# State-space heads: the skip term as a matrix product, the gate in one step, scores in their own bank

## What is computed

```python
cb = jnp.einsum('bclgn,bcsgn->bcgls', cm, bm)                       # scores of a group
y_diag = jnp.einsum('bcgrls,bcsgrp->bclgrp', cb[:, :, :, None] * jnp.exp(seg), xd)
y_off = jnp.einsum('bcqgn,bcgrpn->bcqgrp', cm, h_in) * jnp.exp(a_cs)[..., None]
y = y_f + flip(y_b) + d_skip[:, None] * xs                          # skip term
y = y.reshape(b, l, D_SSD) * jax.nn.silu(z)                         # gate
return rmsnorm(y, norm_w), h_f, h_b
```

## Time and profile before

| | us |
|---|---|
| median of 3 runs | 1427.8 (1423.75 to 1427.95) |
| profiled execution | 1429.21 |
| its span in the trace | 1427.4 |
| busy in the span: TensorE, VectorE, ScalarE, GpSimd | 1308.0, 794.8, 610.0, 88.7 |
| mean granted TensorE clock | 0.972 |

### The profile page before, as it was taken

The page is one execution under the profiler, slowest core; times in us unless marked ns, Lnnn a source line. Parts: engine busy times, 40 slices in busy tenths (PEclk is TensorE's granted clock), DMA queues, the critical chain, the costliest instruction groups (busy, mean ns, idle before and its releaser), DMA issues.

```text
span 1427.4 us, 26314 instructions
## 1 busy us (share of the span) xinstructions
PE 1308.0 (92%) x11170; PEld 1108.6 (78%) x11170; DVE 794.8 (56%) x1220; ACT 610.0 (43%) x947; POOL 88.7 (6%) x69
## 2 busy tenths in 40 slices
PE   7999999999999999999999999899978777877777
PEld 7989698999989988999989999588544334444535
DVE  5558857877467587777458796874222111222214
ACT  6553346444456686454446654763211111121112
POOL 2000000300003100020000000410000000000000
PEclk9999999999999999999999999899998989899999
DMA  9655357554574567445562050468999999999996
GB/s 371 246 206 200 139 216 284 206 190 177 183 312 167 210 251 294 179 177 185 199 240 96 34 236 1 163 266 342 427 428 428 427 429 429 427 429 425 427 428 267
DMA packets 30359, 383.32 MB, mean 269 GB/s; under 512 B 3552, under 2 KB 3728, under 8 KB 7216
## 3 DMA queue, kind: packets, MB, share of 16 engines
q1 hardware_dynamic: 29504, 377.72, 65.2%
q0 software_dynamic: 752, 4.11, 0.7%
HBM read 380.77 MB, written 1.05 MB: 267 GB/s over the span
## 4 chain that ended last, share of the span: by engine, by line
PE 64%; DMA 24%; DVE 6%; ACT 4%; issue 1%; POOL 0%; SPq 0%; DVEq 0%; ACTq 0%; POOLq 0%
PE ps L699 63%; DMA ring<-in_experts 24%; DVE work L2023 2%; DVE w_lo L2011 2%; ACT w_hi L1463 1%; ACT work L1463 1%; ACT HM L1463 1%; DVE work L2011 1%; DVE HM L2011 0%; PE ps L858 0%; DVE SQ L2017 0%; DVE sg_lo L2011 0%; DVE small L2187 0%; DMA ring<-in_dense 0%; ACT L1463 0%
## 5 line engine op out<-in xcount | busy, mean ns | idle before, releaser
L2011 DVE TENSOR_TENSOR w_lo<-ring,w_hi 128x1024 fp32r<-128x1024 f32 (+1 forms) x273 | 338.2, 1245 | 202.9 <-ACT w_hi L1463 202.7
L1463 ACT ACTIVATE w_hi<-ring 128x1024 fp32r<-128x1024 f32 (+1 forms) x273 | 287.0, 1055 | 262.8 <-PE ps L699 258.9
L699 PE MATMUL ps<-in_hi,w_hi 128*128 128x256 f32 x1376 | 388.2, 282 | 11.2 <-DVE w_lo L2011 10.2
L699 PE MATMUL ps<-in_hi,w_lo 128*128 128x256 f32 x1376 | 385.1, 280 | 0.0
L699 PE MATMUL ps<-in_lo,w_hi 128*128 128x256 f32 x1376 | 385.1, 280 | 0.0
L699 PE MATMUL ps<-ring,work 128*32 128x256 f32 (+3 forms) x2520 | 206.0, 460 | 80.9 <-DMA ring<-in_experts 72.6
L699 PEld LDWEIGHTS ps<-in_hi,w_hi 128*128 128x128 f32 x1376 | 261.1, 190 | 15.6 <-issue 13.6
L699 PEld LDWEIGHTS ps<-in_lo,w_hi 128*128 128x128 f32 x1376 | 261.0, 190 | 0.2
L699 PEld LDWEIGHTS ps<-in_hi,w_lo 128*128 128x128 f32 x1376 | 261.1, 190 | 0.0
L699 PEld LDWEIGHTS ps<-ring,work 128*32 128x32 f32 (+1 forms) x2520 | 84.3, 118 | 185.4 <-issue 109.2
L2023 DVE SCALAR_TENSOR_TENSOR X<-ps,mod,X 128x256 f32<-128x256 f32 x136 | 59.0, 479 | 249.7 <-PE ps L699 249.6
(11 more groups left out here) (291 smaller groups left out, 1890.8 us busy)
## 6 DMA issues: line engine op xcount, KB each, us to landing
ring<-in_experts SPq DMA_DIRECT2D x89, 2048.0 KB, 23.1
ring<-in_dense SPq DMA_DIRECT2D x82, 2048.0 KB, 7.5
ring<-in_experts SPq DMA_DIRECT2D x5, 512.0 KB, 20.9
work<-in_experts SPq DMA_DIRECT2D x1, 2048.0 KB, 13.4
ring<-in_dense SPq DMA_DIRECT2D x3, 512.0 KB, 7.2
spare<-in_experts SPq DMA_DIRECT2D x1, 1536.0 KB, 10.6
cst<-in_ret_cst POOLq DMA_DIRECT2D x1, 1280.0 KB, 13.3
cst<-in_experts SPq DMA_DIRECT2D x1, 1280.0 KB, 5.6
```

The costliest lines, as they stand in the source:

```text
L699: i = pe.matmul(o, l, r, start=start, stop=stop)
L1463: x = act.activation(o, i, f, **kw)
L2011: i = dve.tensor_tensor(out=o, in0=x, in1=y, op=op)
```

## The change

- `y`: TensorE first adds the identity times `xs_lat` to the pair's bank, the 12 products accumulate on it. `xs_lat` has been multiplied by `d_skip` in place on ScalarE, eight copies between gating tile 3 and the last two Fourier outputs (`skip_ready`).
- `y_out`: one VectorE step, PSUM times gate into `xs_lat`. Its readers wait for the bank's read count in place of `y_ready`, SP among them.
- Scores: `cb` goes to bank `MODB` with semaphores `cb_full` and `cb_read`; these tiles leave the rotating sequence, so later tiles have lower numbers.
- Squares: `y_square(0)` and `(1)` come after the clamps of heads 8 and 12, `(2)` after head 15; `y_sums(0)` and `(1)` after pairs 4 and 6, `(2)` with `(3)` after the first blocks of the projection.
- States: ScalarE splits the weights first and reads states 0 and 1; VectorE copies states 2 and 3 after its remainders. Pair 0 waits for all four.
- Start-up semaphores `ones_set`, `csil_zero` and `pads_zero` become counts 1, 2 and 3 of `fills`. Their list and three waits are left out of the diff.

```diff
--- before.py
+++ after.py
@@ -216,7 +216,7 @@
         _tiles("state", SG_)
     elif _kind == "mix":
         _seq.append(("mix_out", _i))
-    else:
+    elif _kind != "cb":
         _seq.append((_kind, _i))
 _seq.extend(("mix_out", _i) for _i in (2, 3))
 _tiles("route", 1)
@@ -573,7 +573,8 @@
             hold(0, act2[:, :, :].rearrange("p a b -> p (a b)"), 5)
             hold(1, work[:, 0:2 * FE], 6)
             hold(3, work[:, 2 * FE:3 * FE], 0)
-            sp.wait_ge(s["y_ready"], KX)
+            for j in range(KX):
+                await_read(sp, TILE["y", j])
             hold(2, work[:, 9792:9792 + UNIT], 0)
             sp.wait_ge(s["chunk_used"], MIX0 + 2)
             first_load(5)
@@ -1176,11 +1177,11 @@
                 elif kind == "mix":
                     four_first(i)
                 elif kind == "cb":
-                    t = TILE["cb", i]
-                    await_room(pe, t)
+                    if i:
+                        pe.wait_ge(s["cb_read"], i)
                     for j in range(2):
-                        mm(bank(t)[:, j * T:(j + 1) * T], b_lat[:, i, j * P:(j + 1) * P], c_lat[:, i, :], True, True,
-                           bank_full[t % ROT] if j == 1 else None)
+                        mm(ps[:, MODB, j * T:(j + 1) * T], b_lat[:, i, j * P:(j + 1) * P], c_lat[:, i, :], True, True,
+                           s["cb_full"] if j == 1 else None)
                 elif kind == "row":
                     t = TILE["row", i]
                     await_room(pe, t)
@@ -1193,10 +1194,12 @@
                 else:
                     t = TILE["y", i]
                     await_room(pe, t)
+                    pe.wait_ge(s["skip_ready"], i + 1)
+                    mm(bank(t)[:, 0:T], ident[:, :], xs_lat[:, i, :], True, False)
                     if i == 0:
                         pe.wait_ge(s["xd_ready"], 4)
-                        await_read(pe, TILE["state", 2])
-                        await_read(pe, TILE["state", 3])
+                        for g in range(SG_):
+                            await_read(pe, TILE["state", g])
                     pe.wait_ge(s["m_ready"], 2 * i + 2)
                     pe.wait_ge(s["ce_ready"], 2 * i + 2)
                     for part in range(6):
@@ -1211,10 +1214,10 @@
                                 (xb[:, 1, head], slice(0, T), dm[:, 384 + P:768]),
                                 (state_of[:, lo:lo + SP_], slice(0, T), ce_at[h % 4][:, 0:T]),
                                 (state_of[:, 256 + lo:256 + lo + SP_], slice(0, T), ce_at[h % 4][:, T:2 * T]))[part]
-                            mm(bank(t)[rows, cols], x, y, part == 0, part == 5,
+                            mm(bank(t)[rows, cols], x, y, False, part == 5,
                                bank_full[t % ROT] if part == 5 and h % 2 else None)
-                    if i % 2 and i > 1:
-                        y_sums(i // 2 - 1)
+                    if i in (4, 6):
+                        y_sums(i // 2 - 2)
 
             def logits(j):
 
@@ -1234,6 +1237,7 @@
                 if b and b % BPU == 0:
                     weights("mix_out", b // BPU)
                 if b == KD:
+                    y_sums(2)
                     y_sums(3)
                 n = MIX0 + b // BPC
                 if b % BPC == 0:
@@ -1584,11 +1588,11 @@
                     fn(in_hi[:, c, :], H[:, c, :], ACT.Copy, s["in_hi_ready"])
                 act.wait_ge(s["in_lo_ready"], KD * (i + 1))
 
-            act.wait_ge(s["ones_set"], 1)
+            act.wait_ge(s["fills"], 1)
             fn(small[:, 501:502], ones[:, 0:1], ACT.Identity)
             act.wait_ge(s["ld_gain"], 16)
             next_input(0, "ret_g", ())
-            act.wait_ge(s["csil_zero"], 1)
+            act.wait_ge(s["fills"], 2)
             fn(csil[:, :, 0:2], cut(col("c", 0, 2 * KD), KD, 2), ACT.Silu, s["csil_ready"])
             for j in range(8):
                 weights_hi(chunks_by("ret_g", j))
@@ -1649,7 +1653,7 @@
 
             ffn(0)
             next_input(2, "lru_u", (2,))
-            act.wait_ge(s["pads_zero"], 1)
+            act.wait_ge(s["fills"], 3)
 
             def first_tap(j):
                 act.wait_ge(s["pool_ready"], j + 1)
@@ -1845,7 +1849,8 @@
                 read(TILE["ssd_z", j], pairs(mix, j), ACT.Silu)
 
             def y_square(j):
-                act.wait_ge(s["y_ready"], 2 * j + 2)
+                await_read(act, TILE["y", 2 * j])
+                await_read(act, TILE["y", 2 * j + 1])
                 fn(ysq[j], pairs(xs_lat, j), ACT.Square, s["sq_ready"])
 
             def dft_in(g):
@@ -1880,14 +1885,18 @@
             dft_tokens(2)
             dft_tokens(3)
             gate_tile(3)
+            act.wait_ge(s["wt_ready"], KX + 3 * KB // 2)
+            await_read(act, TILE["turn", KX - 1])
+            for c in range(KX):
+                fn(xs_lat[:, c, :], xs_lat[:, c, :], ACT.Copy, s["skip_ready"], scale=col("d_skip", c))
             dft_out(2)
             dft_out(3)
             await_read(act, TILE["dt_tok", 0])
             for h in range(SH):
                 if h == 2:
-                    for g in range(SG_):
+                    weights_hi(MIX0 + 2)
+                    for g in range(2):
                         read(TILE["state", g], h0[:, g, :])
-                    weights_hi(MIX0 + 2)
                 t = TILE["row", h]
                 await_full(act, t)
                 if h >= 4:
@@ -1899,6 +1908,8 @@
                         fn(dm[:, j * 384:j * 384 + mid], bank(t)[:, j * P:T], ACT.Relu, scale=-1.0, bias=tok6[:, j, h:h + 1])
                         fn(dm[:, j * 384 + mid:(j + 1) * 384], bank(t)[:, T:T + (j + 1) * P], ACT.Relu,
                            s["rl_ready"] if j else None, scale=-1.0, bias=tok6[:, j, SH + h:SH + h + 1])
+                    if h >= 8 and h % 4 == 0:
+                        y_square(h // 4 - 2)
                 else:
                     act.wait_ge(s["cl_ready"], h // 2 + 1)
                 if h >= 2:
@@ -1907,8 +1918,7 @@
                 if h % 2 == 0:
                     act.wait_ge(s["rl_ready"], h // 2 + 1)
                 fn(dm, dm, ACT.Exp, s["dec_ready"], scale=-1.0 if h % 2 == 0 else 1.0)
-                if h >= 7 and h % 4 == 3:
-                    y_square(h // 4 - 1)
+            y_square(2)
             load_norm_tables()
             y_square(3)
             weights_hi(MIX0 + 3)
@@ -2125,8 +2135,8 @@
             def gain_of(i):
                 return lambda c: col("norm_g", i * KD + c)
 
-            dve.memset(ones[:, :], 1.0).then_inc(s["ones_set"], 1)
-            dve.memset(csil[:, :, :], 0.0).then_inc(s["csil_zero"], 1)
+            dve.memset(ones[:, :], 1.0).then_inc(s["fills"], 1)
+            dve.memset(csil[:, :, :], 0.0).then_inc(s["fills"], 1)
             dve.wait_ge(s["ld_gain"], 16)
             for j in range(4):
                 dve.wait_ge(x_in[j], 16)
@@ -2466,25 +2476,21 @@
 
                 t = TILE["y", pair]
                 await_full(dve, t)
-                yx = xs_lat[:, pair, :]
-                stt(yx, yx, col("d_skip", pair), bank(t)[:, 0:T], MUL, ADD, bank_read[t % ROT])
-                await_read(dve, t)
                 if pair == 0:
                     for j in range(4):
                         await_read(dve, TILE["ssd_z", j])
-                tt(yx, yx, mix[:, pair, :], MUL, s["y_ready"])
+                tt(xs_lat[:, pair, :], bank(t)[:, 0:T], mix[:, pair, :], MUL, bank_read[t % ROT])
 
             def masked(g):
 
-                t = TILE["cb", g]
-                await_full(dve, t)
+                dve.wait_ge(s["cb_full"], g + 1)
                 if g >= 2:
                     dve.wait_ge(s["m_ready"], 4 * (g - 1))
-                bk, o = bank(t), cbx[:, g % 2]
+                bk, o = ps[:, MODB, :], cbx[:, g % 2]
                 tt(o[:, 0, 0:T], bk[:, 0:T], smask[:, 0, 0:T], MUL)
                 tt(o[:, 0, T:384], bk[:, 0:P], smask[:, 0, T:384], MUL)
                 tt(o[:, 1, 0:P], bk[:, T + P:2 * T], smask[:, 1, 0:P], MUL)
-                tt(o[:, 1, P:384], bk[:, T:2 * T], smask[:, 1, P:384], MUL, bank_read[t % ROT])
+                tt(o[:, 1, P:384], bk[:, T:2 * T], smask[:, 1, P:384], MUL, s["cb_read"])
 
             def clamped(h):
 
@@ -2508,12 +2514,16 @@
                     if h % 2 == 0:
                         clamped(h + 1)
                 if h % 4 == 0:
-                    await_read(dve, TILE["cb", h // 4])
+                    dve.wait_ge(s["cb_read"], h // 4 + 1)
                 dve.wait_ge(s["dec_ready"], h + 1)
                 dm = decm[:, h % 4, :]
                 tt(dm, dm, cbx[:, h // 4 % 2].rearrange("p a b -> p (a b)"), MUL, s["m_ready"])
                 if h == 1:
                     weights_lo(MIX0 + 2)
+                    for g in range(2, SG_):
+                        t = TILE["state", g]
+                        await_full(dve, t)
+                        dve.tensor_copy(h0[:, g, :], bank(t)).then_inc(bank_read[t % ROT], 1)
```

(10 more changed lines are left out.)

## The result

The changed kernel is slower: 1434.74 us (median of 9 runs, 1431.51 to 1437.51) against 1428.64 us for the kernel before (9 runs), ratio 1.0048, interval 1.0035 to 1.0061. A second measurement gave 1433.02 against 1427.9, ratio 1.0034 (1.0023 to 1.0045). So it costs 5 to 6 us, and the median lies above the predicted range of 1422.0 to 1430.5. The profiled execution took 1434.61 us with a span of 1432.8, 5.4 more than before.

What follows compares the result with a forecast made beforehand. A ring of waits through three engines, not VectorE alone, was taken to bound the head stage. +4.1 us at pair 1, -2.8, -3.0 and +0.5 gave -1.2, so 1426.6 us as median; range 1422.0 to 1430.5.

Steps and rivals of the forecast that it cites:

- the first load: SP's next expert weight load after the last head pair, at 938.95 us before; its shift reaches the end one for one.
- The copies: Eight ScalarE copies after gating tile 3 take 2.9 us; 1.2 us of idle time covers part, head 0 moves 1.7 later.
- the output step: VectorE's step per pair, with the skip step removed and one operand from PSUM, falls from 1.5 to 0.45 us.
- the wait for the scores: Group 1's scores stand behind pair 0 in TensorE's queue, so VectorE now waits for them before its masks.
- the half clock at pair 0: TensorE idles about 2 us ahead of pair 0, its clock falls, and pair 0 takes some 4.0 us, not 2.3.
- Pairs 5 to 7: The last two steps are TensorE's own work back to back: 9.35 us, pair 7 at 935.35 instead of 936.54.
- part (4) of the start: Pair 0, scores, masks and head 3's product, with pair 0 at half clock: pair 1 at 907.0, 4.1 us late.
- the steady path: From head 3's product on, two pairs take 9.1 us against 11.95; the next two also have sums of 0.8.
- the first six identity products: Skip-term products on TensorE for the first six pairs lie in its waits at no cost; without that cover, 2.7 us.
- late start: Start of the head stage gets later: pair 0 by 3.6 us, pair 1 by 4.1 us.
- the ring: Chain of waits through three engines in the steady part, shortened by 2.8 us over two pairs and 3.0 over the next two.
- Rival C: TensorE's waits bring the half clock again at pairs 2 and 4, 3.3 us each: 1433.2 us; chance 0.10.

Runs made afterwards that it cites:

- the order experiment: Changed kernel with the scores of groups 1 to 3 issued by TensorE ahead of pairs 0, 2 and 4 instead of behind them; 1428.83 us, ratio 1.0003.
- both repeats: The kernel before and the changed kernel, each unchanged and profiled again; ratios 0.9996 and 1.0034 against the kernel before.

## Why the prediction was wrong

**Right.** The end follows the first load one for one, give or take 1.3 us (486.8 to 489.4 us from load to end over all profiles). The copies (3.29 us for eight, predicted 2.9), head 0 at 888.90 (1.9 late, predicted 1.7), two state copies in 1.28 (predicted 1.2), the output step at 0.41 (predicted 0.45), the wait for the scores and the half clock at pair 0 all came as said, and pair 0's identity product began at 899.62 with 900.0 predicted. Pairs 5 to 7 took 9.60 us where 9.35 was given.

**Wrong, first: pair 1, part (4) of the start.** Predicted 907.0, measured 909.48. The sum was short by 2.5 us in four terms. The identity product of pair 0 was taken as hidden; it waits for the bank of state 2, so it stands on the path, at half clock: 0.8. Pair 0 took 4.46, not 4.0. The scores took their 1.5 at half clock, not 1.0. Head 3's product took 1.62, not 0.9: as it started late, GpSimd's product (907.34) was already at work.

**Wrong, second: the steady path.** Pairs 1 to 3 were given 9.1 us and took 11.23; pairs 3 to 5 were given 9.9 and took 11.46. Between an odd and the next even pair I laid the path through clamp, exponentials and product, 3.75 us. TensorE's own row from pair to pair is longer: pair 2.3, two rows 1.1, identity 0.6 to 0.8, 4.25 from 920.71 to 924.96, and 5.67 when pair 1 ran slow. I had named the first six identity products as lying in waits; those of pairs 0, 2 and 4 did not, while those of pairs 1, 3 and 5 stood ahead of waits of 1.03, 0.36 and 1.15 us. From pair 4 to pair 5 the sums were 0.97, not 0.8, and head 11's product 1.74, not 0.9, again beside GpSimd.

The sum came out as late start plus shorter ring. The start was right in kind and 2.5 us short. The ring gained 2.1 us over pairs 1 to 5 (11.23 and 11.46 in place of 11.95 and 12.86) where I gave it 5.8 (9.1 and 9.9). Even the 2.1 is clock: in that stretch the half clock cost 3.7 us on the chain before and 1.6 after. Without it, by the same estimate, pairs 1 to 5 took 21.1 us before and 21.1 after (21.2 in both repeats). So the path got no shorter at all, and the step that failed is the ring: I set a sum at full clock, 9.1 and 9.9, against a measured 11.95 and 12.86 that held slow pairs, and booked the difference as a gain of the removed steps and waits. The output step did get shorter by what I said, but the chain of waits no longer passes through it: pair, scores, masks and product are as long a path as the old ring. No run has the shorter step alone, so this last is read from the chains and not tested.

Rival C, the half clock twice more, gave 1433.2 and was near in time, but it is not how it went: the slow stretches fell on pairs 0 and 1, and pairs 2 to 7 ran at full clock. The mechanism I had in hand, scores queued behind a late pair, is the one that the order experiment shows to carry the loss; it stood in my path at all three groups, but too short at group 1, and I set it against a ring that I took for longer than it was.

On the two pages: the Trainium skill (TensorE: Matmul & The Clock Gate, section HAM oscillation) has the engine restart cold after waiting; the 0.50 in 903 to 905 and the 2.3 us of a warmed pair 0 agree. The run with the scores moved alone does not, for it kept the full clock after waits of 1.73 and 2.11 us. The Trainium skill (SBUF — State Buffer, section Who interferes with whom) lets a product with one PSUM operand pass beside GpSimd: the output step at 917.52 took 0.41 us while GpSimd worked, and the products with two SBUF operands took 1.23 to 1.74 in that company.

## What to carry to other kernels

Before work is moved onto an engine to relieve another, lay out the first engine's queue from one long item to the next: that row, with everything that stands in it, may already be the longest path. In a queue that runs in order, put the short item that another engine waits for ahead of the long item that is itself waiting; here moving three sets of scores ahead of their pairs was worth as much as the whole change cost. Before a measured stretch is set against a sum of full-clock rows, take out what its slow rows cost, or the sum wins time that no edit gave it. When an addition has a large idle stretch to go into, check on which side of the next wait it stands: the eight copies missed 5.27 us of idle time by one line, though here the move alone brought nothing clear of noise.

## What had not been expected of the hardware

A late start can cost twice. VectorE's product of 0.94 us took 1.62, 1.74 and 1.94 us (the last in the version with early copies) where, after a wait for the scores, GpSimd's product had begun first, by 0.15 to 0.47 us. At group 2, where GpSimd's began after it, it took 0.95. A wait is not the only way to it: with the scores ahead, other products took 1.69 to 1.70 us beside GpSimd. And a clock kept up at one pair can fall at the next: with four warming products pair 0 ran in 2.3 us and pair 1 in 3.8. The same kernel, run again, had its slow pairs elsewhere (pairs 0 and 1, then pair 0 alone), and its first load moved by 1.8 us.
